# Third mixer's heads in a three-mixer-stage decoder kernel: where squares and skip are added, what the values wait for, and the order of gates and decays

## What is computed

```python
x_in, z = jnp.split(h @ w_in, 2, axis=-1)
x_conv = jax.nn.silu(conv + conv_b)
q = headwise(x_conv, w_q); k = headwise(x_conv, w_k); v = headwise(x_in, w_v)
gates = jnp.concatenate([q, k, v], axis=-1) @ w_if + b_if
hh = mlstm_chunkwise(heads(q) * ML_DH ** -0.5, heads(k), heads(v), i_pre, log_sigmoid(f_pre))
mu = hh.mean(-1, keepdims=True)
var = jnp.mean(jnp.square(hh - mu), axis=-1, keepdims=True)
hn = (hh - mu) * lax.rsqrt(var + LN_EPS) * ln_w
return ((hn + skip * x_conv) * jax.nn.silu(z)) @ w_out
```

## Time and profile before

| | |
|---|---|
| median of 3 runs | 992.75 us (992.52 to 994.33) |
| the profiled execution's own time | 992.56 us |
| its span in the trace | 990.8 us, 16071 instructions |
| TensorE matmul busy | 945.7 us, 95% of the span |
| VectorE busy | 665.9 us, 67% |
| ScalarE busy | 532.3 us, 54% |
| GpSimd busy | 74.9 us, 8% |
| mean granted TensorE clock | 0.991 |
| chain that ended last, share by engine | PE 80%, DVE 10%, ACT 5%, DMA 3%, issue 2% |

### The profile page before, as it was taken

How to read it: one execution, slowest core, us unless ns; L and a number is a source line. 1 busy time by engine, 2 the same in 40 slices (tenths; PEclk the granted TensorE clock), 3 DMA queues, 4 the chain that set the end, 5 groups by cost and what they waited for, 6 DMA issues and landing times.

```text
span 990.8 us, 16071 instructions
## 1 busy us (share of the span) xinstructions
PE 945.7 (95%) x5864; PEld 820.0 (83%) x5864; DVE 665.9 (67%) x1120; ACT 532.3 (54%) x933; POOL 74.9 (8%) x100
## 2 busy tenths in 40 slices
PE   6899999999999899999999998999899999989987
PEld 6899888888888876888888887888788789979875
DVE  4888566454646894575454657975669867498883
ACT  6554465444446664554444447656345664367772
POOL 0100011111100000100000000000021007211100
PEclk9999999999999998999999999999999999999999
DMA  8455656666663532666565553432213565322321
GB/s 306 154 188 170 209 183 225 202 209 204 203 202 107 172 106 77 244 212 211 171 199 182 191 170 107 144 114 84 85 65 128 169 236 192 116 73 90 91 77 47
DMA packets 42812, 156.39 MB, mean 158 GB/s; under 512 B 4957, under 2 KB 5229, under 8 KB 42113
## 3 DMA queue, kind: packets, MB, share of 16 engines
q1 hardware_dynamic: 40320, 146.02, 44.5%
q0 software_dynamic: 1856, 8.51, 2.5%
q10 hardware_dynamic: 576, 1.05, 0.3%
HBM read 154.51 MB, written 1.05 MB: 157 GB/s over the span
## 4 chain that ended last, share of the span: by engine, by line
PE 80%; DVE 10%; ACT 5%; DMA 3%; issue 2%; POOL 0%; SPq 0%; DVEq 0%; ACTq 0%; POOLq 0%
PE ps L706 8%; PE ps L710 8%; PE ps L708 8%; PE ps L546 7%; PE ps L550 7%; PE ps L548 7%; PE ps L497 6%; PE ps L498 6%; PE ps L499 6%; DVE wl L1554 2%; PE ps L1055 2%; DMA raw<-stream_dram 1%; ACT wh L1112 1%; PE ps L1009 1%; PE ps L1030 1%
## 5 line engine op out<-in xcount | busy, mean ns | idle before, releaser
L1554 DVE TENSOR_TENSOR wl<-raw,wh 128x1024 fp32r<-128x1024 f32 x272 | 334.0, 1243 | 125.3 <-ACT wh L1112 68.5
L1112 ACT ACTIVATE wh<-raw 128x1024 fp32r<-128x1024 f32 x176 | 183.6, 1056 | 100.7 <-DMA raw<-stream_dram 70.2
L497 PE MATMUL ps<-hxa,wh 128*128 128x256 f32 x672 | 198.7, 296 | 14.6 <-DVE hxa L1565 8.7
L498 PE MATMUL ps<-hxa,wh 128*128 128x256 f32 x672 | 191.9, 286 | 0.0
L499 PE MATMUL ps<-hxa,wl 128*128 128x256 f32 x672 | 191.7, 285 | 0.0
L497 PEld LDWEIGHTS ps<-hxa,wh 128*128 128x128 f32 x672 | 130.6, 194 | 26.4 <-issue 17.8
L706 PE MATMUL ps<-wh,hxa 128*128 128x512 f32 x352 | 139.1, 395 | 0.9 <-DVE hxa L1575 0.9
L710 PE MATMUL ps<-wl,hxa 128*128 128x512 f32 x352 | 137.3, 390 | 0.0
L708 PE MATMUL ps<-wh,hxa 128*128 128x512 f32 x352 | 137.0, 389 | 0.0
L546 PE MATMUL ps<-wh,y 128*128 128x512 f32 x336 | 132.8, 395 | 1.3 <-DVE y L1644 0.7
L548 PE MATMUL ps<-wh,y 128*128 128x512 f32 x336 | 131.4, 391 | 0.0
(11 more groups left out here) (348 smaller groups left out, 1272.3 us busy)
## 6 DMA issues: line engine op xcount, KB each, us to landing
raw<-stream_dram SPq DMA_DIRECT2D x272, 512.0 KB, 3.9
biasm<-bias_dram POOLq DMA_DIRECT2D x12, 192.0 KB, 3.9
w<-w_dram POOLq DMA_DIRECT2D x1, 2048.0 KB, 9.2
mlw<-mlw_dram POOLq DMA_DIRECT2D x1, 1056.0 KB, 6.8
x0T<-xT_dram ACTq DMA_DIRECT2D x4, 256.0 KB, 7.5
x<-x_dram SPq DMA_DIRECT2D x1, 1024.0 KB, 6.7
mem<-memT_dram SPq DMA_DIRECT2D x1, 1024.0 KB, 5.8
grow<-rows_dram POOLq DMA_DIRECT2D x2, 512.0 KB, 3.8
```

Of the source, the lines that this page charges most:

```text
L497: pe.matmul(o, wh[:, w_s, w_cols], act[hi], start=start, stop=False, skip_group_check=True)
L498: pe.matmul(o, wh[:, w_s, w_cols], act[lo], start=False, stop=False, skip_group_check=True)
L1112: act.activation(wh[:, v % RING, :], raw[:, v % RAW, :], ACT.Copy).then_inc(wh_ready, 1)
L1554: dve.tensor_tensor(wl[:, s % RING, :], raw[:, s % RAW, :], wh[:, s % RING, :].bitcast(F32), ALU.subtract).then_inc(wl_ready, 1)
```

## The change

The diff, with the new semaphore `ml_sq_added` in the list of names left out:

```diff
@@ -430,6 +430,9 @@
             if c < 2:
                 return zpre[:, c, :]
             return zlo[:, c, :] if c < 8 else zhi[:, c - 8, :]
+
+        def zy_of(c):
+            return zpre[:, c, :] if c < 2 else z_y[:, c % 2, :]
 
 
         NEEDS = {}
@@ -848,21 +851,20 @@
             pe.matmul(ps[0:36, 3, 0:T], gsel[:], gq[:], start=True, stop=True).then_inc(gsum_ready, 1)
             ml_scores(1)
             project(PM["z", 2], hxa)
+            project(PM["z", 3], hxa)
             pe.wait_ge(g_ready, 1)
             for st in range(2):
                 mm = pe.transpose(ps[:, 3, T + 4 * st:T + 4 * st + 4], g_g[0:4, st * P:st * P + P], ident[0:4, 0:4])
             mm.then_inc(g_turned, 1)
-            project(PM["z", 3], hxa)
             pe.wait_ge(v_centred, ML_HEADS)
             pe.wait_ge(g_em_ready, 1)
-            pe.wait_ge(gcol_ready, 1)
 
             def ml_values(h):
                 pe.wait_ge(ml_weighed, h + 1)
                 pe.wait_ge(v_centred, h + 1)
                 if h >= 1:
 
-                    pe.wait_ge(ml_done, h)
+                    pe.wait_ge(ml_normed, h)
                 s = h_s[:, h % 2, :]
                 pe.matmul(ps[:, 4, 0:T], ones[:], s[:, 0:T], start=True, stop=False)
                 pe.matmul(ps[:, 4, P:T], ones[:], s[:, T:T + P], start=False, stop=True)
@@ -876,10 +878,8 @@
 
             def ml_var(h):
                 pe.wait_ge(ml_den_ready, h + 1)
-                pe.wait_ge(ml_squared, h + 1)
-                for c in range(4):
-                    mm = pe.matmul(ps[:, 4, T:2 * T], ones[:], h_sq[:, c, :], start=(c == 0), stop=(c == 3))
-                mm.then_inc(ml_sq_summed, 1)
+                pe.wait_ge(ml_sq_added, h + 1)
+                pe.matmul(ps[:, 4, T:2 * T], ones[:], h_sq[:, 0, :], start=True, stop=True).then_inc(ml_sq_summed, 1)
 
             def gate_chunks(a, b):
                 for c in range(a, b):
@@ -898,9 +898,12 @@
             for h in range(ML_HEADS):
                 if 0 < h < ML_HEADS - 1:
                     ml_scores(h + 1)
+                if h == 0:
+                    gate_chunks(*Z_BEFORE[h])
                 if h + 1 < ML_HEADS:
                     ml_rows(h + 1)
-                gate_chunks(*Z_BEFORE[h])
+                if h >= 1:
+                    gate_chunks(*Z_BEFORE[h])
                 ml_values(h)
                 gate_chunks(*Z_BEHIND[h])
                 if h == ML_HEADS - 1:
@@ -1387,11 +1390,11 @@
                     act.activation(skipx[:, b, :], xconv[:, b, :], ACT.Copy, scale=col("skip", b))\
                         .then_inc(skip_ready, 1)
 
+            act.wait_ge(v_done, ML_CH)
+            act.activation(gq[:], ps[0:64, 3, 0:T], ACT.Copy).then_inc(gq_copied, 1)
             for c in range(2):
                 act.wait_ge(proj_taken, PM["z", c].n + 1)
                 act.activation(z_of(c), z_of(c), ACT.Silu).then_inc(silu_ready, 1)
-            act.wait_ge(v_done, ML_CH)
-            act.activation(gq[:], ps[0:64, 3, 0:T], ACT.Copy).then_inc(gq_copied, 1)
             act.wait_ge(g_negabs, 1)
             link(act.activation(g_e[:], g_n[:], ACT.Exp))
             act.activation(g_e[:], g_e[:], ACT.Ln, bias=eps[0:4, 2:3]).then_inc(g_ln, 1)
@@ -1422,25 +1425,33 @@
             def gated(a, b):
 
                 for c in range(a, b):
-                    high(z_y[:, c % 2, :], c % 4, M_ML + c)
+                    high(zy_of(c), c % 4, M_ML + c)
                     if 2 <= c + 1 < ML_CH:
                         gate_silu(c + 1)
                     ahead(PM_OUT["out", c])
 
             decays(0)
             for h in range(ML_HEADS):
+                if h == 0:
+                    gate_chunks(*Z_BEFORE[h])
                 if h + 1 < ML_HEADS:
                     decays(h + 1)
-                gate_chunks(*Z_BEFORE[h])
+                if h >= 1:
+                    gate_chunks(*Z_BEFORE[h])
                 if h == ML_HEADS - 1:
-                    gated(0, 2)
+                    for c in range(2):
+                        high(zy_of(c), c, M_ML + c)
                 act.wait_ge(ml_summed, h + 1)
                 if h >= 1:
-                    act.wait_ge(ml_sq_summed, h)
+                    act.wait_ge(ml_done, h)
                 for b in range(2):
                     e = act.activation(h_sq[:, 2 * b:2 * b + 2, :], ps[:, 6 + b, :], ACT.Square)
                 e.then_inc(ml_squared, 1)
                 gate_chunks(*Z_BEHIND[h])
+                if h == ML_HEADS - 1:
+                    gate_silu(2)
+                    ahead(PM_OUT["out", 0])
+                    ahead(PM_OUT["out", 1])
                 if h == ML_HEADS - 1:
                     gated(2, 6)
                 act.wait_ge(ml_var_ready, h + 1)
@@ -1977,23 +1988,28 @@
                             dve.wait_ge(y_ready, Y_ML + c - 1)
                         if c % 4 == 0:
                             dve.wait_ge(ml_done, c // 4 + 1)
-                        dve.tensor_tensor(z_y[:, c % 2, :], z_of(c) if c < 2 else z_s[:, c % 2, :], skipx[:, c, :],
-                                          ALU.mult)\
+                        dve.tensor_tensor(zy_of(c), z_of(c) if c < 2 else z_s[:, c % 2, :], skipx[:, c, :], ALU.mult)\
                             .then_inc(prod_ready, 1)
                     if c >= 1:
-                        low_part(z_y[:, (c - 1) % 2, :], (c - 1) % 4, Y_ML + c - 1)
+                        low_part(zy_of(c - 1), (c - 1) % 4, Y_ML + c - 1)
                         if c < ML_CH:
                             ahead(PM_OUT["out", c - 1])
 
-            gate_chunks(2, 4)
+            gate_chunks(2, 3)
             decays(0)
+            gate_chunks(3, 4)
             weigh(0)
             for h in range(ML_HEADS):
+                if h == 0:
+                    gate_chunks(*Z_BEFORE[h])
                 if h + 1 < ML_HEADS:
                     decays(h + 1)
-                gate_chunks(*Z_BEFORE[h])
                 if h == ML_HEADS - 1:
-                    gated(0, 2)
+                    gated(0, 1)
+                if h >= 1:
+                    gate_chunks(*Z_BEFORE[h])
+                if h == ML_HEADS - 1:
+                    gated(1, 2)
                 if h + 1 < ML_HEADS:
                     weigh(h + 1)
 
@@ -2003,6 +2019,9 @@
                 e = dve.scalar_tensor_tensor(out=h_a[:], in0=ps[:, 4, 0:T], scalar=-1.0, in1=h_a[:],
                                              op0=ALU.mult, op1=ALU.max)
                 e.then_inc(ml_den_ready, 1)
+                dve.wait_ge(ml_squared, h + 1)
+                link(dve.tensor_tensor(h_sq[:, 0:2, :], h_sq[:, 0:2, :], h_sq[:, 2:4, :], ALU.add))
+                dve.tensor_tensor(h_sq[:, 0, :], h_sq[:, 0, :], h_sq[:, 1, :], ALU.add).then_inc(ml_sq_added, 1)
                 dve.wait_ge(ml_den_ready, h + 1)
                 link(dve.reciprocal(h_r[:], h_a[:]))
                 gate_chunks(*Z_BEHIND[h])
@@ -2029,10 +2048,10 @@
                 e.then_inc(ml_normed, 1)
                 if h == ML_HEADS - 1:
                     gated(9, 10)
-                    dve.wait_ge(ml_normed, h + 1)
-                    dve.wait_ge(skip_ready, ML_CH)
-                    xc = skipx[:, 4 * h:4 * h + 4, :]
-                    dve.tensor_tensor(xc, xc, h_sq[:], ALU.add).then_inc(ml_done, 1)
+                dve.wait_ge(ml_normed, h + 1)
+                dve.wait_ge(skip_ready, ML_CH)
+                xc = skipx[:, 4 * h:4 * h + 4, :]
+                dve.tensor_tensor(xc, xc, h_sq[:], ALU.add).then_inc(ml_done, 1)
             gated(10, ML_CH + 1)
 
 
@@ -2263,21 +2282,12 @@
             pool.wait_ge(ssq_ready, 2 * Q_ML + 2)
             pool.dma_start(gsel[:], gsel_d).then_inc(gsel_landed, 16)
 
-            def skip(h):
-
-                pool.wait_ge(skip_ready, ML_CH)
-                pool.wait_ge(ml_normed, h + 1)
-                xc = skipx[:, 4 * h:4 * h + 4, :]
-                nc.gpsimd.tensor_tensor(xc, xc, h_sq[:], ALU.add).then_inc(ml_done, 1)
-
             for h in range(ML_HEADS):
 
                 pool.wait_ge(ml_decayed, h + 1)
                 d = h_w[:, h % 2, :].rearrange("p (i c) -> p i c", c=T)[:, :, 0:P]
                 nc.gpsimd.affine_select(out=d, in_=d, compare_op=ALU.is_ge, fill=0.0, base=0,
                                         pattern=[[0, 2], [1, P]], channel_multiplier=-1).then_inc(ml_masked, 1)
-                if h >= 1:
-                    skip(h - 1)
 
             pool.wait_ge(prod_ready, M_N)
             pool.dma_start(w1[:], w1_d).then_inc(w1_landed, 16)
```

## The result

The changed kernel takes 996.21 us, the median of 18 runs (993.88 to 1000.21); the kernel before takes 993.23 in as many runs beside it. The ratio is 1.0035, with a 95% interval of 1.0022 to 1.0048: slower by 2 to 5 us, where 995.6 was forecast in a range of 990.5 to 998.0.

What follows compares the result with a forecast made beforehand. TensorE was taken to lead VectorE's nearly as long loop by about 0.3 us in 17, with VectorE's longer loop using up the gains. 992.56 + 1.9 (output 1 later) + 1.0 (clock) = 995.5, 995.6 on the median's scale; range 990.5 to 998.0.

Steps and rivals of the forecast that it cites:

- The loop on VectorE: Denominator marks in the heads 19.4 and 17.8 us apart, 10.7 to the norm, using up the gains of 4.6 and 5.2.
- The last head: Products end at 761.0, denominator at 766.3, low part of output 1 done at 770.9; output 1 starts 1.9 us later.
- The start: Gates and chunks reordered before the first values: 4.6 us gained, with 0.8 us of new wait for chunk 2's bank.
- rival 2: Two clock falls, or one already in the 0.8 us wait for chunk 2's bank: 997.4 us, chance 0.14.
- The clock under the outputs: TensorE's pauses between 759 and 768 lower the clock: 1.0 us lost, between ends of nothing and 3.4.
- the crossing: Last head: VectorE waits for output 4's weight unit, which ScalarE makes behind squares, table load and silu; denominator at 766.3.
- Rival 1: No fall of the clock that costs, under idle time or with TensorE's pauses cut up: 994.7 us, chance 0.25.
- Rival 3: Weight unit of output 4 is there when VectorE comes at 761.3; output 1 starts 2.1 us earlier: 990.6, chance 0.12.
- Rival 4: TensorE stays the bound in the heads, so 5.2 + 4.6 + 1.6 us show: 981.3 us, chance 0.03.
- Rival 5: Whole kernel: the parts cancel or the edits do nothing net: 992.7 us, chance 0.05.
- Rival 6: A VectorE price too low: the 3.08 us remains, or the table load costs its drain: 997.2 us, chance 0.03.

Runs made afterwards that it cites:

- first experiment: Changed kernel with ScalarE making the weight unit of output 4 behind the two high parts, ahead of the last squares: 993.25 us, ratio to the kernel before 1.0004.
- the skip on GpSimd: Changed kernel with the skip of heads 0 to 2 on GpSimd again, values still waiting for the banks alone: 994.87 us, ratio to the kernel before 1.0031.
- Take-first: Changed kernel with VectorE's take of chunk 2 ahead of its wait for the turned gates: 995.21 us, ratio to the kernel before 1.0025.
- part 1 alone: Kernel before with only gq first, chunk 3 ahead of the turn, chunk 4 ahead of the rows of head 1: 988.26 us, ratio 0.9937.
- kept-busy run: Changed kernel with eight useless matmuls behind output 0, in TensorE's pause ahead of the last sum of squares: 995.87 us, ratio to the kernel before 1.0028.
- four matmuls: Changed kernel with the sum of squares by four matmuls on TensorE and no additions on VectorE: 990.03 us, ratio to the kernel before 0.9970.
- part 1 undone: Changed kernel with gates, chunks and decays at the start in the order of before: 1001.7 us, ratio to the kernel before 1.0093.

## Why the prediction was right, step by step

*The loop on VectorE.* Forecast from mark to mark 19.4 and 17.8 us, and 10.7 to the norm: measured 19.28, 17.56 and 10.49. Additions: 0.69 and 0.42 us, as taken.

*The last head.* From the norm to the end of the second product 6.3 forecast, 759.93 - 753.63 = 6.3. From there to the denominator 5.3 forecast, 765.20 - 759.93 = 5.27. From there to the low part of output 1 4.1 forecast, 3.98 measured. The moved weight unit gives 3.0 us back (first experiment). ScalarE's table load took 1.28 us and silu began 1.30 us behind its start: the further 1.38 us that the Trainium skill ("ScalarE: Activation LUTs", "What ACT_TABLE_LOAD costs") adds for a drain don't appear; here the measurement decides. The lock of which the Trainium skill speaks ("SBUF — State Buffer", "Who interferes with whom"), for a VectorE instruction with two SBUF inputs beside a GpSimd one that reads SBUF, agrees with the trace twice: the weight subtraction took 3.08 us beside GpSimd's skip in the kernel before and 3.39 in the run with the skip on GpSimd, 1.22 by itself.

*The start was the term that was missized.* I wrote that a pause of 1.3 us does no harm to the clock "so I count none", and a gain of 4.6 us. The profiled execution has a pause of 1.18 us and not 0.8, and the clock at 0.91 and 0.89 over the two stretches, chunk 4 taking 701.60 - 697.03 = 4.6 us:

```profile
697.03 0.39 PE L500 MATMUL ps<-hxa,wh 128*128 128x256 f32 x1 [1.18 <-DVE zlo L1618]
...
701.60 0.69 PE L844 MATMUL ps<-g_M,sel 4*128 4x256 f32 x2
```

Gain 2.9. That was named in rival 2, "already in the 0.8 us wait for chunk 2's bank". The same length of pause left the clock up at other places (1.34 us before, at 741), so the length of one pause doesn't say it. Take-first removed pause and fall together. All this is read from profiled executions; the runs of part 1 alone gain 4.4 to 8.1 us, which takes in the 4.6, and why they gain more than their trace is open.

*The clock under the outputs.* I took 1.0 us between 0 and 3.4. The kept-busy run gives 1.7 for the pause ahead of the last sum. With the start, the stage in the profiled execution loses 4.8 us and not 2.9; the runs show 3.0 in the median. What happened lies between the forecast and rival 2.

*What was luck.* In the trace output 1 starts 2.9 us late and not 1.9: 1.7 us too much counted for the start, 0.6 us too much for VectorE's loop and 0.1 for the last head work against each other. Behind it another 1.9 us are lost and not 1.0. That the median came out within 0.6 us of 995.6 is therefore better than the sum deserved. The denominators too look better hit than they are. I named 706.8, 726.2, 744.0 and 766.3 and they stand at 706.30, 725.58, 743.14 and 765.20, but this execution came to the stage 2.3 us earlier; measured from there they are 1.8, 1.7, 1.4 and 1.2 us late. The clock at 1.0 between 699 and 708 didn't come, and the fall at 746 wasn't forecast. The mechanisms held: VectorE's loop uses up both gains, and the crossing holds VectorE.

*The rivals.* Rival 1 (no fall that costs): fell, 0.62 between 766 and 775. Rival 3 (the crossing doesn't hold VectorE): fell, 3.80 us of idle. Its size is still of use: with the crossing undone the kernel would be at 990.6, I wrote; it was 993.3, and 1.7 us of the difference are the fall at chunk 4, which I had not counted. Rival 4 (TensorE bound): fell with the four matmuls. Rival 5 fell by the interval of the ratio. Rival 6 (a VectorE price too low): fell, the weight subtraction of 756.58 took 1.22 us and not 3.08, and the load brought no drain.

Left open: why the median with four matmuls fell 6 us where the stage shortened by 3.3, and what in the order of pauses makes the clock fall in one place and not in the other.

## What to carry to other kernels

When two engines' programs are reordered, write down for each instruction that is waited for what now stands ahead of it on its own engine: a weight unit of 1 us placed behind squares, a table load and a silu cost 3 us. Before work is moved onto an engine that looks two thirds busy, time the loop through it from mark to mark: VectorE at 67% was within 0.3 us of being the bound, since it waits for ScalarE in that loop, and of 2.2 us more per head 1.8 and 1.4 us came out at the next mark. And a wait that is only shortened may still bring the clock down; freeing the bank before the wait (one moved take) gave 2.7 us.

## What the runs showed that was not expected

A pause of 1.18 us ahead of chunk 4 came with a fall to the lower level in each of the six profiles that had it at that place (the changed kernel, and those with the weight unit moved, four matmuls, part 1 alone, the skip on GpSimd, TensorE kept busy), and in none of the five that had part 1 without the pause; pauses of 1.3 to 1.5 us elsewhere in the kernel before came with none. The pause of 2.64 us ahead of the sum of head 2 came with a fall in three profiles (the changed kernel, the weight unit moved, TensorE kept busy) and with none in two that had it as well (take first, part 1 undone). So neither length nor place of a pause alone tells whether the clock falls behind it. The run with part 1 undone lost 3.4 us of clock behind its stall of 2.67 us, the kernel before 1.7 behind the same stall. The kernel before itself varies from 988.5 to 996.1 us over 23 executions on one chip, and the mean granted clock goes with it: 0.995 in the fastest, 0.988 in the slowest. So a change of 0.3% in this kernel needs many executions; a trace shows where the time of its one execution went.
